# Expert layers of a hybrid diffusion step: the down product in full precision from the landed weights

## The reference

```python
def hier_moe(h, w_group_router, w_expert_router, w1, w3, w2):
    ...
    hid = jax.nn.silu(jnp.einsum('nd,edf->nef', x, w1)) * jnp.einsum('nd,edf->nef', x, w3)
    out = jnp.einsum('nef,efd->nd', hid * gates[:, :, None].astype(hid.dtype), w2)
```

## Time and profile before

| | |
|---|---|
| device time, median of 3 runs | 2075.46 us (2069.21 to 2075.76) |
| the profiled execution: its own time | 2068.9 us |
| its span | 2067.1 us |
| PE busy | 1827.7 us (88%) |
| DVE busy | 1047.9 us (51%) |
| ACT busy | 800.5 us (39%) |
| mean granted TensorE clock | 0.939 of full |

### The profile page before, as it was taken

The page is one execution under the profiler, slowest core; times in us unless marked ns, Lnnn a source line. Parts: engine busy times, 40 slices in busy tenths (PEclk is TensorE's granted clock), DMA queues, the critical chain, the costliest instruction groups (busy, mean ns, idle before and its releaser), DMA issues. The chain is left out here.

```text
span 2067.1 us, 28080 instructions
## 1 busy us (share of the span) xinstructions
PE 1827.7 (88%) x11240; PEld 1513.8 (73%) x11240; DVE 1047.9 (51%) x1563; ACT 800.5 (39%) x1085; POOL 256.5 (12%) x242
## 2 busy tenths in 40 slices
PE   6799899999999996899849998989999999848892
PEld 2798555679999983677628975556799999737671
DVE  3322566762323456787672226477522334557784
ACT  2311261663112321677662203516521223227773
POOL 0101510000000000253220033100000000004430
PEclk8799999999999998899958999999999999969996
DMA  9113301312222418898762123021111225249984
GB/s 362 57 60 85 110 27 57 120 50 65 79 62 92 163 72 299 328 353 320 279 252 84 50 68 136 22 102 63 62 62 62 92 72 194 82 158 352 348 317 187
DMA packets 127958, 299.90 MB, mean 145 GB/s; under 512 B 10792, under 2 KB 53352, under 8 KB 119144
## 3 DMA queue, kind: packets, MB, share of 16 engines
q1 hardware_dynamic: 110664, 264.15, 35.2%
q0 software_dynamic: 9792, 20.99, 2.7%
q10 hardware_dynamic: 7392, 13.19, 2.2%
HBM read 283.25 MB, written 29.72 MB: 151 GB/s over the span
## 5 line engine op out<-in xcount | busy, mean ns | idle before, releaser
L1887 PE MATMUL pair<-hT_r,mid_r 128*128 128x320 f32 x768 | 237.3, 309 | 0.0
L1887 PE MATMUL pair<-mid_r,r_r 128*128 128x512 f32 (+1 forms) x528 | 193.9, 367 | 23.7 <-DVE hT_r L1679 23.6
L1887 PE MATMUL pair<-r_r,ring_r 128*128 128x320 f32 x832 | 211.8, 309 | 2.2 <-DVE ring_r L1254 2.2
L1669 DVE TENSOR_TENSOR ring_r<-ring,mid_r 128x2048 fp32r<-128x2048 f32 x68 | 155.7, 2292 | 59.1 <-ACT mid_r L1072 59.0
L1887 PE MATMUL pair<-ysT_r,mid_r 128*128 128x256 f32 (+1 forms) x768 | 172.1, 315 | 14.7 <-issue 9.5
L1887 PE MATMUL pair<-mid_r 128*128 128x320 f32 x576 | 178.9, 311 | 1.6 <-issue 1.6
L1887 PE MATMUL pair<-r_r,mid_r 128*128 128x256 f32 (+2 forms) x576 | 180.2, 313 | 0.0
L1887 PE MATMUL pair<-mid_r,ring_r 128*128 128x320 f32 x576 | 178.0, 309 | 0.0
L1969 PE MATMUL pair<-cst,mid 128*128 128x128 f32 x748 | 119.7, 300 | 64.1 <-DVE mid L1200 32.0
L1969 PEld LDWEIGHTS pair<-cst,mid 128*128 128x128 f32 x748 | 92.6, 153 | 111.3 <-DVE mid L1200 39.7
L1482 DVE TENSOR_TENSOR r<-pair,r 128x640 f32<-128x640 f32 x48 | 39.5, 823 | 252.3 <-PE pair L1887 252.3
(11 more groups left out here) (276 smaller groups left out, 3827.7 us busy)
## 6 DMA issues: line engine op xcount, KB each, us to landing
ring<-in_w_mod SPq DMA_DIRECT2D x23, 2048.0 KB, 8.8
ring<-in_w_gate SPq DMA_DIRECT2D x34, 1024.0 KB, 5.9
ring<-in_w_up SPq DMA_DIRECT2D x34, 1024.0 KB, 8.4
ring<-in_w_down SPq DMA_DIRECT2D x34, 1024.0 KB, 9.4
ring<-in_w_in SPq DMA_DIRECT2D x24, 1024.0 KB, 7.0
ring<-in_w_in SPq DMA_DIRECT2D x8, 2048.0 KB, 10.8
ring<-in_w_branch SPq DMA_DIRECT2D x12, 1024.0 KB, 5.1
ring<-in_w_out SPq DMA_DIRECT2D x8, 1024.0 KB, 5.3
```

Source lines behind the costliest of these rows:

```text
L1669: V.tensor_tensor(w13_parts[s][1][:, own], w13[s][:, own], w13_parts[s][0][:, own], ALU.subtract).then_inc(w13_ready, 1)
L1887: return nc.tensor.matmul(out, lhsT, rhs, start=first, stop=last, skip_group_check=True)
```

## The change

The gate and up products stay split. The down product becomes a plain 32-bit product (`mm`) of the turned inner values and the landed down weights. ACT no longer casts the down weights, DVE no longer subtracts them, and DVE's remainder of the inner values goes too: ACT copies the turned inner values into a plain buffer `hidT`, and this copy alone signals `down_ready`. PE's `down` now waits on the landing of the down weights itself (`down_in`). The casts that are counted by `rounded` fall from five to three a block, so the counts that DVE waits on change.

```diff
...
         w13_parts = [(view(mid_r, s * 4096, 4096), view(ring_r, (1 - s) * 6144, 4096)) for s in range(2)]
-        w2_parts = [(view(ysT_r, s * 2048, 2048), view(ring_r, (1 - s) * 6144 + 4096, 2048)) for s in range(2)]
...
         xg_parts = [(view(r1_r, (2 + s) * D, D), view(hT_r, s * D, D)) for s in range(2)]
-        hid_parts = [(view(hT_r, 2 * D + s * FF, FF), view(hT_r, 2 * D + (2 + s) * FF, FF)) for s in range(2)]
+        hidT = view(hT, 2 * D, 2 * FF, a=2)
         yo = view(r1, 10 * D, 2 * D, a=2)
...
         up_in = [sem(f"up_in{i}") for i in range(2)]
-        rounded, w13_ready, w2_ready = sem("rounded"), sem("w13_ready"), sem("w2_ready")
+        rounded, w13_ready = sem("rounded"), sem("w13_ready")
         hid_turned, down_ready = sem("hid_turned"), sem("down_ready")
...
-                def round_down(s, rnd):
-
-                    act.wait_ge(down_in[s], rnd * 16 + 16)
-                    nc.scalar.copy(w2_parts[s][0], w2s[s]).then_inc(rounded, 1)
-
                 def round_tokens(b, s):
...
-                def round_hidden(b, s):
+                def hidden_turned(b, s):
                     act.wait_ge(hid_turned, b + 1)
-                    nc.scalar.copy(hid_parts[s][0], pair[1][:, s * 512:s * 512 + FF]).then_inc(rounded, 1)
+                    nc.scalar.copy(hidT[:, s, :], pair[1][:, s * 512:s * 512 + FF]).then_inc(down_ready, 1)
...
                         round_tokens(b + 1, 1 - s)
-                    round_down(s, rnd)
-                    round_hidden(b, s)
+                    hidden_turned(b, s)
                     if not (first and s == 0):
...
-                def remainder_down(s, count):
-
-                    dve.wait_ge(rounded, count)
-                    V.tensor_tensor(w2_parts[s][1], w2s[s], w2_parts[s][0], ALU.subtract).then_inc(w2_ready, 1)
-
                 def remainder_tokens(s, count):
...
                     V.tensor_tensor(hid[:, s, :], sil[:, s, :], pair[1][:, s * 512 + FF:s * 512 + 2 * FF], ALU.mult).then_inc(hid_ready, 1)
-
-                def remainder_hidden(s, count):
-
-                    dve.wait_ge(rounded, count)
-                    V.tensor_tensor(hid_parts[s][1], pair[1][:, s * 512:s * 512 + FF], hid_parts[s][0], ALU.subtract).then_inc(down_ready, 1)
...
                     if not (last and s):
-                        remainder_tokens(1 - s, b * 5 + 6)
-                    remainder_down(s, b * 5 + (4 if last and s else 7))
-                    remainder_hidden(s, b * 5 + (5 if last and s else 8))
+                        remainder_tokens(1 - s, b * 3 + 6)
                     if not last:
-                        remainder_up(s, b * 5 + 9)
+                        remainder_up(s, b * 3 + 7)
...
-                def down(b, s):
-
-                    pe.wait_ge(w2_ready, b + 1)
+                def down(b, s, rnd):
+
+                    pe.wait_ge(down_in[s], rnd * 16 + 16)
                     pe.wait_ge(down_ready, b + 3)
...
                         for k in range(FT):
-                            last = three_products(out[:, j * 512:(j + 1) * 512], [x[:, k * P:(k + 1) * P] for x in hid_parts[s]],
-                                                  [x[:, k * D + j * 512:k * D + (j + 1) * 512] for x in w2_parts[s]], k == 0, k == FT - 1)
+                            last = mm(out[:, j * 512:(j + 1) * 512], hidT[:, s, k * P:(k + 1) * P],
+                                      w2s[s][:, k * D + j * 512:k * D + (j + 1) * 512], k == 0, k == FT - 1)
                     last.then_inc(y_filled, 1)
...
                     if not (first and s == 0):
-                        down(b - 1, 1 - s)
+                        down(b - 1, 1 - s, rnd - 1 + s)
                     turn_hidden(b, s)
...
                     block(n_more * 2 + (2 + s), s, n_more + 1, False, True)
-                down(n_more * 2 + 3, 1)
+                down(n_more * 2 + 3, 1, n_more + 1)
                 pe.wait_ge(y_filled, n_more * 2 + 6)
...
```

## The result

The changed kernel takes 2084.44 us (median of 20 runs, 2069.5 to 2095.0), the kernel before 2074.83 in the runs beside it (20 runs, 2063.16 to 2085.59). The ratio is 1.0046 with a 95% interval of 1.0029 to 1.0063: slower by 9.6 us, where 2073 and "no change" were forecast. A second series gave 1.0057 (1.0031 to 1.0082).

A forecast was written before the change was run, and what follows sets the result against it. DMA and the loop of request, landing, casts and subtractions, up product were taken to set the pace, PE close behind. +3.6 - 4.0 - 1.7 = -2.1 us from the 2075.46 median gave 2073, range 2058 to 2090.

The forecast's parts named there:

- +3.6 us: Expert blocks: about 13 of 34 start `up` some 0.6 us late; half pass the delay on, 6 x 0.6.
- -4.0 us: PE's clock: the longer down product shortens three waits for inner values, sparing 1.5 falls of 2.7 us each.
- forecast 0.70: PE in each block: the plain down product takes 3.5 us, 0.70 us longer than the split one.
- a request that comes 0.6 us later lands no later: Weight transfers: where the DMA engines are full (413 GB/s), sending 0.6 us late does not delay landing.
- Six of 16 blocks are of this kind: Blocks where no PE wait before `up` covers the longer down product: 16 less 10 waits, so about 13 of 34.
- 0.87: PE's average idle time in us per block, in the first stretch of seven blocks taken as 10.57 us each.
- The layer's end, -1.7 us: First layer's last block: down product starts earlier, so the output copy comes at 1031.8, not 1033.49; second layer 0.
- I cost all of it at nothing: Inside the block loop, removing ACT's casts (64.9 us) and DVE's subtractions (77.8 us) and small remainders gains nothing.
- A: Rival, chance 0.18: PE becomes the bound and the down product's length enters the period; 2099 for all blocks, 2087 for half.
- under 0.70 us of idle PE time: Point ahead of `up` in a block from which the down product's length goes into the period.
- blocks over 10.8: Sign in the first stretches: blocks taking over 10.8 us would mean PE had become the bound.
- B: Rival, chance 0.09: freed ACT and DVE let the DMA run full; up to -32 us, 2044, a third of it 2065.

The follow-up runs named there:

- the kernel that sends early: Changed kernel with separate remainder buffers, requesting the next gate and up weights when the remainders are done, not after the up product: 2054.95 us, 0.9912 of the kernel before.
- the kernel with other places: Changed kernel with gate and up remainders in buffers of their own and down weights landing in two pieces, requests sent as before: 2084.96 us, 1.0052.
- the early kernels: The kernel that sends early (2054.95 us), and the same with twelve float32r matmuls on a constant table as down product (2066.34 us, two blocks more).
- the product alone: Kernel before with the plain down product, its casts and subtractions kept but their results unused by PE: 2085.13 us, 1.0034; again 2085.24 us, 1.0044.
- the control: Kernel before, same matmuls, second depth tile's product overwritten by the first's, so 36 blocks in place of 34: 2097.79 us, 1.0102.
- the two controls: Kernel before and changed kernel, each with the second depth tile's product overwritten by the first's, so 36 blocks: 2097.79 us (1.0102) and 2102.05 us (1.0146).
- casts alone: Changed kernel with twelve float32r matmuls on a constant table in place of the plain down product, 36 blocks: 2092.09 us, 1.0070 of the kernel before.
- the control of the change: Changed kernel, all four plain products issued, second depth tile's overwritten by the first's, so 36 blocks: 2102.05 us, 1.0146 of the kernel before.

## Why the prediction was wrong

**Two terms failed: "+3.6 us" ("I let half of them pass") and the clock's "-4.0 us".** The first came out nearly twice as large, and the second with the other sign.

**The passed-on delays.** Each step before this term held. PE's shortest block grew by 0.67 us (9.33 to 10.00; forecast 0.70), of which the down product has 0.61 (2.83 to 3.44) and the transposes ahead of it 0.08, and blocks without cover are there. The step behind it, that at full DMA engines "a request that comes 0.6 us later lands no later", doesn't hold over a round. A delay of `up` delays its send, and the engines run dry later, as at 925 to 930 us. The turn of a buffer (send, landing, 5.8 us of casts and subtractions, `up`) is as long as the two blocks that it may take, so nothing makes the lost rate up. That this loop holds the blocks up is shown by the kernel that sends early: its mean block is 10.22 us against 11.25 in the kernel with other places, with hardly a wait or a fall left. That the 0.67 us is passed on by the same way is a reading of the round above, and the early kernels bear it out in one layer of two. Measured: 0.18 to 0.21 us a block, the falls taken off, so 6 to 7 us in the loop where 3.6 was forecast. By the times, the product alone costs 7.1 and 9 us, with intervals of 6 us either way, falls and layer ends included.

**"Six of 16 blocks are of this kind"** was also too few. The count took a block as covered when PE had waited about 0.8 us before. After the change the same count gives ten: PE waited 6 times for the token remainder in 850 to 1020 us, for 6.1 us, where it was 10 times and 8.1 us. The kernel mixes blocks in which PE runs without a pause with longer ones, and an average wait is not slack that every block may use. The average itself was read too large: seven blocks are 72.7 us and PE is busy 67.44 of them, so it stood idle 0.75 us a block, not 0.87.

**The clock, -4.0 us.** The argument was that a longer product shortens the waits. It does inside one block, but the waits come from weights that land late, and a late `up` sends for the next ones late. PE's waits for the inner values, 850 to 1020 us, went from 5.4 us in four to 4.1 in four, and the longest stayed: 2.16 us above, 2.20 in the earlier trace rows. What the slow `up` products took is 8.5 us on average before and 10.9 after, by two profiles each, so about +2.4 where -4.0 was forecast, more of a miss than that of the first term. Three falls in the one trace that the forecast had was also the low end: a second profile of that kernel has six.

**The layer's end, -1.7 us, held where it applied.** After the change the first layer's inner values were turned at 1035.89, the product began at 1036.73 and the copy at 1040.47:

```profile
1035.89 0.38 PE L2265 MATMUL pair<-cst,r 128*128 128x128 f32 x2
1036.73 3.70 PE L1868 MATMUL opair<-ring,hT 128*128 128x512 f32 x8 [0.46 <-ACT hT L1086]
```

That is 4.58 us from turn to copy, 7.01 before, forecast 4.6. From last `up` to last copy: 15.3 before, 13.6 after. But the gain was the clock's: an end with a fall takes 15.2 or 15.3, one without 13.6 or 13.7, in either kernel. Before, one end of two had a fall in each profile (in the second one it was the second layer's); after, none in the first profile, and the second layer's in the second. So 1.7 us is what the first pair shows, and the second pair shows 0.2.

**"I cost all of it at nothing"** held in the loop: ACT 61 us and DVE 88 us less (forecast 65 and 92), and two direct comparisons see no gain. The place was another than forecast: ACT doesn't wait longer for the up weights but for PE, which turns the inner values behind its down product. In the round shown, landing to `up` stayed at 5.8 us. The layer ends do gain from it: with twelve matmuls and no casts they take 24.4 us against the control's 29.1.

**The sum.** With what was measured it is 6 to 7 us passed on, about 2.4 of falls and -0.2 to -1.8 at the layer ends, 7 to 9 in all; the measured change is 9.6, with 6 to 13 as its interval.

**Of the rivals,** A was the nearest, in its half form: 2087 forecast, 2084.4 measured. It named the right cause, the product's length going into the period. That half of the blocks came so near was in part luck: 0.2 of each block's 0.67 us is passed on by the loop when the falls are taken off, and the falls add to it. Its turning point ("under 0.70 us of idle PE time") lay close, since the idle time was 0.75 and not 0.87, and the sign "blocks over 10.8" came out at 11.2 in the first stretch, 11.4 (80 / 7) in that of the second layer. I gave it 0.18 because of the 0.87. That the later send matters was in the text as a doubt and not as a rival. B is refuted, since freed engines sent nothing sooner; sending early gave 2055, of B's size by another cause.

**What stays open.** The 0.2 of 0.67 us isn't derived, only measured, and the two controls alone would give 0.06. By the times of whole runs the share is wider: the change itself allows 0.3 to 0.6 of the added PE time; casts alone against the control of the change gives two thirds, with an interval that begins at 0.35. Whether the change adds falls of the clock isn't settled. Early sending in the kernel before wasn't tried: its casts of the down weights lie where the separate remainders would have to go.

## What to carry to other kernels

Where two buffers are refilled only when their consumer ends, the consumer's lateness is also the transfer's lateness: an engine at 93% of the period is part of the bound, and mean idle time must not be counted as slack. Compare the mean block with the engine's shortest one, and price a longer and a shorter piece of work apart: here the longer one cost, and the shorter gave the loop nothing. Before work is traded between engines in such a loop, look at what frees the buffer. Here, sending one `up` product (5.6 us) earlier was worth 30 us, more than leaving out half of the down product gave (22 us); and the room for it was what the otherwise losing change had set free.

## What the runs showed of the hardware

- A plain 32-bit product of 128x512 stands in the trace as two matmuls of 0.43 us, the split one as three of 0.23. Four plain ones took 3.44 us, four split ones 2.83: the split form is the cheaper one on PE, so leaving it out makes PE longer even as it empties two other engines.
- Eight transposes ahead of a plain product took 0.87 us (927.65 to 928.52), and 0.79 ahead of a split one (882.12 to 882.91 in the trace of before).
- With a fall of the clock `up` took 6.9 to 7.2 us in most cases and 7.7 to 8.5 in a few. In the fall shown above the matmuls are 0.43 us apart up to 924.00 and 0.23 from there on: 3.5 us of this `up` ran at the lower level, 1.2 GHz. It followed waits of 2.16 and 0.78 us with 0.44 us of transposes between them.
- In the early version the DMA engines kept 364 GB/s for 143 us in the first layer (860 to 1003 us) and 369 GB/s for 70 us in the second (1868 to 1938 us).
